# A branch prefetch hint at the head of each engine's loop over the experts

## The reference, cut to what matters

```python
def ec_moe(x, w_router, w_gate, w_up, w_down):
    T = B * S
    C = max(1, CAPACITY_FACTOR * T // N_EXPERTS)          # 32 and 64 tokens, 16 experts
    aff = jax.nn.softmax((xt @ w_router).astype(jnp.float32), axis=-1)
    gates, idx = lax.top_k(aff.T, C)                      # each expert chooses its C tokens
    xe = xt[idx]
    h = jax.nn.silu(jnp.einsum('ecd,edf->ecf', xe, w_gate)) * jnp.einsum('ecd,edf->ecf', xe, w_up)
    ye = jnp.einsum('ecf,efd->ecd', h, w_down) * gates[..., None].astype(x.dtype)
    out = jnp.zeros_like(xt).at[idx.reshape(-1)].add(ye.reshape(-1, D))
```

## Time and profile before

| | |
|---|---|
| median of 3 runs | 2866.32 us (2864.72 to 2871.19) |
| profiled execution, its own time | 2863.62 us |
| its span in the trace | 2861.6 us |
| TensorE busy | 2727.4 us (95%) |
| VectorE, ScalarE, GpSimd busy | 963.9, 612.1, 584.0 us |
| moved by DMA | 603.44 MB, 211 GB/s over the span |
| first matmul of the expert loop's first jump back | 1974.06 us, after 4.04 us of idle time |
| last matmul's work ends | about 2846 us |

### The profile page before, as it was taken

One profiled execution on the slowest core, in us unless ns is written; L12 is line 12 of the kernel. 1 busy time (PEld: TensorE's weight loads), 2 busy tenths in 40 slices (PEclk: granted clock), 3 DMA queues, 4 the chain that ended last, 5 costly groups with the idle time before them and its releaser, 6 DMA issues. The chain is left out here.

```text
span 2861.6 us, 53476 instructions
## 1 busy us (share of the span) xinstructions
PE 2727.4 (95%) x18871; PEld 1372.9 (48%) x18871; DVE 963.9 (34%) x2089; ACT 612.1 (21%) x1838; POOL 584.0 (20%) x969
## 2 busy tenths in 40 slices
PE   8999999999999999999898999999999999999997
PEld 4544455556676676676563455332333233333332
DVE  1135444431364464464654235311111111111100
ACT  4100355521322322413310111311111111111100
POOL 1445111102222322323510000211111111211111
PEclk9999999999999999999998999999999999999999
DMA  7664100021220221210516448799999999999996
GB/s 248 216 220 149 56 29 30 22 91 31 73 58 29 70 60 37 61 31 23 191 68 260 162 143 341 317 411 406 405 397 407 383 406 383 409 380 395 394 412 230
DMA packets 170387, 603.44 MB, mean 211 GB/s; under 512 B 16527, under 2 KB 81895, under 8 KB 116455
## 3 DMA queue, kind: packets, MB, share of 16 engines
q1 hardware_dynamic: 163175, 587.08, 53.3%
q0 software_dynamic: 6912, 12.59, 2.5%
HBM read 553.65 MB, written 45.98 MB: 210 GB/s over the span
## 5 line engine op out<-in xcount | busy, mean ns | idle before, releaser
L2749 PE MATMUL psum<-wbuf 128*32 128x512 f32 x2976 | 347.4, 608 | 35.8 <-issue 34.0
L2749 PE MATMUL psum<-x,wbuf 128*32 128x512 f32 x3024 | 340.0, 592 | 0.0
L1458 PE MATMUL psum<-xT,wbuf 128*128 128x512 f32 x720 | 336.8, 606 | 0.3 <-PEq L831 0.3
L718 POOL COPY wbuf<-xT 128x16 f32 x533 | 114.5, 215 | 782.5 <-issue 430.8
L2749 PEld LDWEIGHTS psum<-wbuf 128*32 128x32 f32 x2976 | 113.0, 112 | 259.0 <-issue 259.0
L2749 PEld LDWEIGHTS psum<-x,wbuf 128*32 128x32 f32 x3024 | 114.7, 110 | 211.9 <-issue 211.9
L718 DVE COPY wbuf<-xT 128x16 f32 x500 | 95.0, 191 | 339.9 <-issue 339.0
L1458 PEld LDWEIGHTS psum<-xT,wbuf 128*128 128x128 f32 x720 | 132.1, 192 | 128.1 <-issue 122.4
L2766 PE MATMUL psum<-x,hT 128*32 128x512 f32 x1584 | 177.9, 592 | 0.0
L718 ACT COPY wbuf<-xT 128x16 f32 x503 | 111.3, 221 | 275.7 <-issue 272.5
L2766 PE MATMUL psum<-wbuf,hT 128*32 128x512 f32 x1488 | 167.5, 592 | 2.1 <-DVE ye L2836 2.1
(11 more groups left out here) (328 smaller groups left out, 3386.8 us busy)
## 6 DMA issues: line engine op xcount, KB each, us to landing
x<-in_w_down SPq DMA_DIRECT2D x66, 1024.0 KB, 11.2
wbuf<-in_w_gate SPq DMA_DIRECT2D x65, 1024.0 KB, 9.3
wbuf<-in_w_up SPq DMA_DIRECT2D x65, 1024.0 KB, 12.0
x<-in_w_gate SPq DMA_DIRECT2D x63, 1024.0 KB, 9.7
x<-in_w_up SPq DMA_DIRECT2D x63, 1024.0 KB, 11.9
wbuf<-in_w_down SPq DMA_DIRECT2D x62, 1024.0 KB, 10.8
wbuf<-in_w_in SPq DMA_DIRECT2D x16, 2048.0 KB, 9.2
wbuf<-weight_sums SPq DMA_DIRECT2D x16, 2048.0 KB, 9.2
```

Of the source, the lines that this page charges most:

```text
L718: last = copy(k.xeT[:, half, :, t:t + 1], k.mixT[:, :, cols][:, :, bass.ds(r, 1)])
L1458: last = nc.tensor.matmul(ps[:, b, 0:SS_], wg[:, m % 2, d, h * P:(h + 1) * P], k.xT[:, d, SP_:T], start=(d == 0), stop=(d == KD - 1))
L2749: last = nc.tensor.matmul(ps[32 * j:32 * j + 32, g, :].rearrange("p (x c r) -> p x c r", x=2, r=32), xeT[:, half, q, 32 * g:32 * g + 32], ...
```

## The change

Each of the five loops is opened with an option of `Fori` that marks the loop's closing compare-and-branch: a branch prefetch hint, one instruction, is put as the first instruction of each turn and names the jump back to the head that stands at the turn's end. The bodies, the waits, the order and the number of turns stay as they are.

```diff
@@ SP
-                with sync.Fori(0, NE - 1) as e:
+                with nc.Fori(0, NE - 1, engines=[sync.engine], hint_back_edge=True) as e:
@@ TensorE
-                with pe.Fori(0, NE // 2 - 1) as pair:
+                with nc.Fori(0, NE // 2 - 1, engines=[pe.engine], hint_back_edge=True) as pair:
@@ ScalarE
-                with act.Fori(0, NE // 2 - 1) as pair:
+                with nc.Fori(0, NE // 2 - 1, engines=[act.engine], hint_back_edge=True) as pair:
@@ VectorE
-                with dve.Fori(0, NE // 2 - 1) as pair:
+                with nc.Fori(0, NE // 2 - 1, engines=[dve.engine], hint_back_edge=True) as pair:
@@ GpSimd
-                with pool.Fori(0, NE // 2 - 1) as pair:
+                with nc.Fori(0, NE // 2 - 1, engines=[pool.engine], hint_back_edge=True) as pair:
```

## The result

| | before | after |
|---|---|---|
| median, 4 runs each | 2865.52 us (2864.19 to 2871.19) | 2830.6 us (2826.3 to 2831.7) |
| ratio, 95% interval | | 0.9869 (0.9854 to 0.9885) |
| profiled execution: time, span | 2863.62, 2861.6 us | 2831.7, 2829.9 us |
| start of the span to TensorE's first jump | 1970.02 | 1966.04 |
| first jump to the loop's end (12 experts) | 791.5 | 757.6 |

The change takes 35 us, 1.3%, against 34 forecast, and the time lies in the range (2826 to 2854). The last three rows split the difference of the two spans, 31.7 us, into three parts of which I had written down only the middle one: 33.9 us come from the loop, 6.2 are lost behind it, and 4.0 are gained ahead of the first jump, where nothing was changed: TensorE's first turn already begins at 1837.5 us, against 1841.5 before.

What follows compares the result with a forecast made beforehand. TensorE bounds the kernel, with weight transfers next. Jumps cost 49.9 us; TensorE alone would save 37.6, transfers allow 34.6, the smaller saving counts, with friction 34: 2866.3 - 34 = 2832.3 us, range 2826 to 2854.

Steps and rivals of the forecast that it cites:

- The cost of the jumps: TensorE's expert loop: six jumps back cost 49.9 us, 8.3 each, rather than the 34.0 of the waits' row.
- First stretch: TensorE's idle time at each jump, 4.04 to 3.38 us while the head's code is fetched: goes entirely.
- Second stretch: TensorE's idle time 15 matmuls behind each jump, read as a code fetch: 2.0 us a jump remain, bounds 0 to 2.8.
- Transfers: Weight loads, late next: 63.7 us an expert against TensorE's 61.80, so 15.3 us of waits, allowing a saving of 34.6.
- reserve: How far weight transfers are ahead of TensorE's need before the first jump: 8.3 to 12 us, taken as 10.
- the rate of 411 GB/s: Sign in the profile after: DMA rate over whole turns rises to about 410 GB/s, from 400 and 394.
- SP's gap behind the first jump: Sign in the profile after: SP's 12 us without issuing loads behind a jump shrinks to near 5.
- The other engines at nothing: Loops of SP, ScalarE, VectorE and GpSimd: their hints gain zero, since their stalls are not on the path.
- A: Rival, weight transfers: the core averages only 400 GB/s, saving 16 us, 2840 to 2854 us; chance 0.13.
- B: Rival, TensorE's jumps: first stretches go but the second grows, saving 12 to 21 us, 2845 to 2854; chance 0.08.
- C: Rival, TensorE's loop: the hint does nothing over so long a turn, time stays 2866 us; chance 0.14.
- D: Rival, TensorE's loop head: the mark's fetch goes ahead of the following code's, 37 us slower, 2903 us; chance 0.05.

Runs made afterwards that it cites:

- e7: e3 with half of the down weights' columns not loaded, matmuls kept: 2812.1 us, ratio to the kernel before 0.9801.
- e6: The kernel before with TensorE's loop head placed at the first instruction of a 256-instruction fetch block, no hint: 2842.2 us, ratio 0.9909.
- e3: The change with TensorE's seven turns written out instead of looped, other engines still hinted: 2827.9 us, ratio to the kernel before 0.9859.
- e4: The change with TensorE's loop head placed at instruction 0 of a fetch block: 2826.5 us, ratio to the kernel before 0.9863.
- e5: The change with TensorE's loop head placed at instruction 100 of a fetch block: 2831.1 us, ratio to the kernel before 0.9866.
- e1: The kernel before with the hint on TensorE's loop alone: 2842.1 us, ratio 0.9912.
- e8: e3 with no hint on any engine: 2840.9 us, ratio to the kernel before 0.9905.
- e2: The change without TensorE's hint, so hints on SP, ScalarE, VectorE and GpSimd only: 2866.8 us, ratio to the kernel before 0.9999.
- e12: The change with TensorE's mark set ahead of the turn's last unit, 5.2 us ahead of the jump: 2832.9 us, ratio to the kernel before 0.9879.
- e11: The kernel before with half of each down-weight load left out: 2871.3 us, a single time.

## Why the prediction was right, point by point

**The cost of the jumps.** Read as turn lengths, 49.9 us and not the 34.0 of the waits' row. e7, where nothing holds TensorE, has 741.6 us for 12 experts against 791.5: 49.9. The clock behind the stretches is part of the price.

**First stretch.** It went entirely, as worked out.

**Second stretch.** I called it a code fetch, which e6 shows, and forecast 2.0 us a jump with the clock. The turns without a wait for transfers lost 1.8 (125.42 - 123.6) and the first 2.3. The 2.0 was the middle of wide bounds (0 to 2.8), so that it came this close is in part luck.

**Transfers.** This was the term that set the forecast. Its 15.3 us are for the 13.3 experts left at the first jump; for the loop's 12 the same working gives 1.9 x 12 - 10 = 12.8, so 754.4 us. The change took 757.6, e3, e4 and e5 756.0, 755.8 and 757.5: somewhat more than the sum. The rate in it, 63.7 us an expert, is what the last turns of e3 show, and its 14.4 us leave a reserve of 8.4 (1.9 x 12 = 22.8, less 14.4), near the 10 that I took and inside 8.3 to 12. Of the signs I had named, the rate of 411 GB/s came true. The waits for transfers are 2.9 us in 3 times, not the 5 to 15 in most turns, since what TensorE idles at jumps counts for the transfers too, as the sum itself said; and SP's gap behind the first jump shrank from 12 us to 7.0 (1966.80 to 1973.84), not to near 5. The change's 16.0 us over 741.6 are 1.8 to 2.3 at each jump, and only in the last two turns 2.2 to 2.4 more each.

**The other engines at nothing.** This step was wrong. I asked whether their stalls lie on the path, and they don't. I didn't ask what unmarked jumps on these engines cost the resource that was to become the bound, though my own sum carried all code as "under 0.1" MB an expert by its bytes. The pairs with e1 and e8 show 12.3 us of the loop, 64.8 us an expert in e8 against 63.7. The total came out right all the same, because my 63.7 is the figure of the kernel with the hints, but I hadn't aimed at that: the rates came from 55 us of the kernel before with 5 packets of q14 in them, near the loop's mean of 87 in 791.5. The same working would have given 63.7 for e1 as well, where it is wrong by 12 us. That it fell on the right one of the two is luck; no run explains why.

**The exit.** It is missing from the sum. The prediction knew the loop's end only as a fall-through of 0.076 us; the block behind it wasn't there, which cost a stretch of 3.4 us and its clock, 6.2 us in all against before. In the profiled pair it was partly made up by the 4.0 us ahead of the loop that go with the execution; so part of the closeness of 31.9 us (profiled) to the forecast 34 is chance.

**The rivals.** A (transfers at 400 GB/s) falls with 411 over the whole loop. B (the second stretch grows) falls with 1.6 us. C, the hint without effect on TensorE, falls with 0.35 us, and with it, for a marked jump, the sentence of the Trainium skill (Runtime: NRT & Kernel Launch, Instruction fetch mechanics) that prefetch is purely sequential; its rule that a taken branch to a target outside the window stalls agrees with the 6.0 us of the unmarked jump. D (the mark displaces a fetch and makes it slower) had the wrong place but not the wrong idea: the mark does take the place of a fetch, that of the block behind the jump, and only the exit pays for it.

## What to carry to other kernels

A loop whose row has a compare-and-branch of several us is worth a mark on the engine that sets the time; cost it by turn lengths, not by the wait's row, and then ask which resource is late next and sum that one to the end. Once a shared resource binds, the loop of an engine far off the path can still matter: mark it too. Where the head and the jump stand in their fetch blocks can be worth as much as the mark: here placement alone (e6, 0.9909) gave as much as the mark on TensorE alone (e1, 0.9912).

## What the runs showed of the hardware

- An unmarked jump of TensorE over 2332 instructions takes 5.7 to 6.0 us (before, e2, e6), a marked one 0.35, a late-marked one 0.77 (e12); the mark takes 0.036 us.
- The fetch goes by blocks of 256 instructions (55 packets for 13,860 instructions in e3): with the head at 0 the second stretch vanished (e6), and with the jump some 28 instructions into its block the marked branch still took 3.3 us (e4).
- A mark at the head replaces the fetch of the block behind the jump's (60 packets against 66) and costs a stretch of 3.4 us at the exit; a mark 5.2 us ahead of the jump adds a fetch and costs nothing there, but the stretch behind each jump is 1.8 to 2.2 us with it, in place of 1.5 to 1.7 (e12).
- Without marks on SP, ScalarE, VectorE and GpSimd the loop has 87 more code packets of 8 KB and takes 12.3 us more where transfers bind, and no more where they don't (e2, by the timed runs). The packets' bytes would be 1.7 us at 425 GB/s. Whether the rest is the packets' too, or the later copies and scatters, no run shows.
- Halving the rows of a third of the weight loads left the unmarked jump at 6.1 to 6.5 us (e11). The packet of 16 KB itself takes 0.9 to 1.0 us of that.
